# Sums of weights for the fast block products: made by adding transfers in device memory and loaded, in place of VectorE additions

## The reference

```
n2 = rms_norm(h)                      # 512 x 1024
a  = relu(n2 @ w_in) ** 2             # w_in 1024 x 4096
h  = h + a @ w_out                    # w_out 4096 x 1024
```

## Time and profile before

| what | value |
|---|---|
| median of 3 runs | 1870.49 us (1870.12 to 1870.89) |
| the profiled execution, its own time | 1871.36 us |
| its span | 1869.6 us |
| TensorE busy | 1858.5 us (99%) |
| VectorE busy | 1369.3 us (73%) |
| ScalarE busy | 944.1 us (50%) |
| GpSimd busy | 87.4 us (5%) |
| moved by DMA | 179.34 MB, mean 96 GB/s |

### The profile page before, as it was taken

One profiled execution on the slowest core, in us unless ns is written; L12 is line 12 of the kernel. 1 busy time (PEld: TensorE's weight loads), 2 busy tenths in 40 slices (PEclk: granted clock), 3 DMA queues, 4 the chain that ended last, 5 costly groups with the idle time before them and its releaser, 6 DMA issues.

```text
span 1869.6 us, 28250 instructions
## 1 busy us (share of the span) xinstructions
PE 1858.5 (99%) x10603; PEld 1546.0 (83%) x10603; DVE 1369.3 (73%) x1870; ACT 944.1 (50%) x1206; POOL 87.4 (5%) x84
## 2 busy tenths in 40 slices
PE   9999999999999999999999999999999999999998
PEld 7788878888888887877888898988778788989897
DVE  7767775677357667556577898987788658789887
ACT  6392464555133344444543554555667744445464
POOL 0010021000000021000100000000110010000000
PEclk9999999999999999999999999999999999999999
DMA  6223122332322234222233223234232133233321
GB/s 242 90 85 125 44 68 68 104 98 68 112 90 91 74 105 134 68 82 68 90 99 98 96 92 113 92 112 149 88 104 71 59 101 102 82 107 99 105 91 68
DMA packets 146802, 179.34 MB, mean 96 GB/s; under 512 B 3581, under 2 KB 140669, under 8 KB 144256
## 3 DMA queue, kind: packets, MB, share of 16 engines
q1 hardware_dynamic: 143296, 160.44, 26.4%
q0 software_dynamic: 3104, 17.10, 2.9%
q10 hardware_dynamic: 288, 0.26, 0.0%
HBM read 173.48 MB, written 2.20 MB: 94 GB/s over the span
## 4 chain that ended last, share of the span: by engine, by line
PE 92%; DVE 5%; ACT 2%; DMA 1%; issue 0%; DVEq 0%; SPq 0%; ACTq 0%
PE bank L1059 22%; PE bank L1061 22%; PE bank L1060 22%; PE bank L1496 4%; PE bank L1498 4%; PE bank L1497 4%; PE bank L1187 2%; PE bank L1801 2%; PE bank L1783 1%; PE bank L1193 1%; DVE w_lo L2061 1%; DMA raw<-in_mlp_w_out 1%; PE bank L1672 1%; PE bank L1673 1%; PE bank L1674 1%; DVE w_lo L1897 1%
## 5 line engine op out<-in xcount | busy, mean ns | idle before, releaser
L1059 PE MATMUL bank<-n_hi,w_hi 128*128 128x512 f32 x1054 | 424.7, 403 | 1.3 <-DVE w_lo L1897 1.3
L1061 PE MATMUL bank<-n_hi,w_lo 128*128 128x512 f32 x1054 | 417.9, 396 | 0.0
L1060 PE MATMUL bank<-n_lo,w_hi 128*128 128x512 f32 x1054 | 416.7, 395 | 0.0
L1891 ACT ACTIVATE w_hi<-raw 128x2048 fp32r<-128x2048 f32 (+2 forms) x115 | 215.0, 1870 | 342.1 <-PE bank L1061 337.5
L1897 DVE TENSOR_TENSOR w_lo<-raw,w_hi 128x2048 fp32r<-128x2048 f32 (+2 forms) x121 | 271.2, 2241 | 105.5 <-ACT w_hi L1891 103.4
L1060 PE MATMUL bank<-ff_lo,w_hi 128*128 128x512 f32 x752 | 297.2, 395 | 0.0
L1061 PE MATMUL bank<-ff_hi,w_lo 128*128 128x512 f32 x688 | 273.0, 397 | 0.0
L1059 PE MATMUL bank<-ff_hi,w_hi 128*128 128x512 f32 x688 | 271.5, 395 | 1.0 <-DVE ff_lo L2199 0.8
L1059 PEld LDWEIGHTS bank<-n_hi,w_hi 128*128 128x128 f32 x1054 | 198.0, 188 | 54.2 <-issue 5.0
L1060 PEld LDWEIGHTS bank<-n_lo,w_hi 128*128 128x128 f32 x1054 | 198.1, 188 | 48.9 <-issue 2.9
L1061 PEld LDWEIGHTS bank<-n_hi,w_lo 128*128 128x128 f32 x1054 | 197.9, 188 | 46.6
(11 more groups left out here) (455 smaller groups left out, 3111.1 us busy)
## 6 DMA issues: line engine op xcount, KB each, us to landing
raw<-in_mlp_w_in SPq DMA_DIRECT2D x32, 1024.0 KB, 5.4
raw<-in_mlp_w_out SPq DMA_DIRECT2D x32, 1024.0 KB, 5.1
raw<-in_w_up SPq DMA_DIRECT2D x22, 1024.0 KB, 5.0
raw<-in_w_units SPq DMA_DIRECT2D x14, 1024.0 KB, 4.8
raw<-in_a_w_qkv SPq DMA_DIRECT2D x12, 1024.0 KB, 5.1
raw<-in_b_w_qkv SPq DMA_DIRECT2D x12, 1024.0 KB, 5.1
b_bias<-bias_table POOLq DMA_DIRECT2D x16, 448.0 KB, 4.5
raw<-in_w_down SPq DMA_DIRECT2D x8, 768.0 KB, 4.4
```

What stands on the lines that cost most here:

```text
L1059: nc.tensor.matmul(b[:, :], w_hi[:, j % 2, cols], hi, start=start, stop=False)
L1060: nc.tensor.matmul(b[:, :], w_hi[:, j % 2, cols], lo, start=False, stop=False)
L1061: return nc.tensor.matmul(b[:, :], w_lo[:, j % 2, cols], hi, start=False, stop=final)
L1891: act.activation(w_hi[:, s, cols], raw[:, s, cols], ACT.Copy).then_inc(hi_ready, 1)
```

## The change

The two MLP weight matrices are handed over in blocks (`in_blocks`, on the host): for each unit a contiguous 128 x 2048 array whose row holds four blocks of 512 columns, in the order of `BLOCK_ORDER` (A21, A11, A12, A22 as (tile, far) pairs (1, 0), (0, 0), (0, 1), (1, 1)). A unit's row in memory is then 8 KB in one run, where it was 8 runs of 1 KB.

POOL gets a new piece of work, `weight_sums`, in two sets of 15 units. The first set stands behind `norm_pool(1)`, ahead of `attention_a_pool`; the second behind `norm_pool(4)`, ahead of `attention_b_pool`. For each unit it issues five transfers from device memory to device memory: two copies of two blocks (512 KB each), an adding transfer of two blocks, another of two blocks, and one of one block (256 KB). The four stages of a unit are spread over four steps, each step holds the stages of up to four units, and POOL waits at the start of a step until all transfers of the step before have landed. A set has 18 steps.

SP loads, for each of the 30 units, three blocks of the unit (768 KB, `raw[:, :, SEQ:4*SEQ]`) and its four sums (1024 KB) straight into `s_parts`. The load of the sums waits on SP for the sums to be made and for the place to be free. VectorE's three sum instructions are gone, and some signs are turned in the remaining additions (a subtraction in place of an addition, or `scalar_tensor_tensor` with -1). S1 and S4 change places. The plain products of these matrices read their columns in the new order.

```diff
+BLOCK_ORDER = ((1, 0), (0, 0), (0, 1), (1, 1))
+def in_blocks(w, rows, cols):
+    v = w.reshape(2, rows, KD // 2, 2, P, cols, 4, 2, P).transpose(0, 1, 5, 6, 4, 7, 3, 2, 8)
+    v = np.stack([v[:, :, :, :, :, tile, far] for tile, far in BLOCK_ORDER], 5)
+    return v.reshape(32, P, UNIT)
...
+        def block_loads(sp, ph):
+            m, is_out = block_phases[ph]
+            for j in range(4):
+                u = j if not is_out else DOWN if j == 2 else None
+                sp.wait_ge(lo_ready, ph.u0 + j - 1)
+                if u is None:
+                    sp.dma_start(raw[:, j % 2, :].rearrange("p (k n) -> p k n", n=GC).unsqueeze(1),
+                                 ph.view[:, j:j + 1, :, :]).then_inc(w_loaded[j % 2], 16)
+                    continue
+                sp.dma_start(raw[:, j % 2, SEQ:4 * SEQ], t["mlp_out" if is_out else "mlp_in"][4 * m + j, :, SEQ:4 * SEQ]).then_inc(
+                    w_loaded[j % 2], 16)
+                row = SUM_ROW[m, u]
+                sp.wait_ge(sums_made, 16 * sums_issued[row + 3, SUM_SETS[m // 4][0]])
+                if u == 0:
+                    sp.wait_ge(at("piece_lo"), split_count[m - 1, "operand", OPERANDS - 1] if m % 4 == 1 else split_count[m - 1, "S14", DOWN])
+                elif u == 1 and m % 4 > 1:
+                    piece_used(sp, m - 1, ("S3", DOWN))
+                elif u > 1:
+                    sp.wait_ge(at("piece_lo"), split_count[m, "S14", 2 if u == DOWN else u - 2])
+                i = sums_place(u)
+                sp.dma_start(s_parts[i], t["weight_sums"][row]).then_inc(sums_loaded[i], 16)
...
+            def copied(row):
+                v, to = source(row), sums(row)
+                pool.dma_start(to[:, 0:2, :], v[:, 1:2, :].broadcast_to([P, 2, SEQ])).then_inc(sums_made, 16)
+                pool.dma_start(to[:, 2:4, :], v[:, 2:4, :]).then_inc(sums_made, 16)
+            def first_added(row):
+                pool.dma_start(sums(row)[:, 1::2, :], source(row)[:, 0:1, :].broadcast_to([P, 2, SEQ]), accum_op=ALU.add).then_inc(sums_made, 16)
+            def second_added(row):
+                pool.dma_start(sums(row)[:, 0:4:2, :], sums(row)[:, 3:4, :].broadcast_to([P, 2, SEQ]), accum_op=ALU.add).then_inc(sums_made, 16)
+            def third_added(row):
+                pool.dma_start(sums(row)[:, 2:3, :], source(row)[:, 1:2, :], accum_op=ALU.add).then_inc(sums_made, 16)
+            for step in range(first, last + 3):
+                if step > first:
+                    pool.wait_ge(sums_made, 16 * sums_issued[step - 1, first])
+                for back, part in enumerate((copied, first_added, second_added, third_added)):
+                    if first <= step - back < last:
+                        part(step - back)
+            pool.wait_ge(sums_made, 16 * sums_issued[last + 2, first])
...
             norm_pool(pool, 1)
+            weight_sums(pool, *SUM_SETS[0])
             pool.wait_ge(at("bias_stored"), 16)
             attention_a_pool(pool)
             norm_pool(pool, 4)
+            weight_sums(pool, *SUM_SETS[1])
             attention_b_pool(pool)
...
-            own_dve(dve, dve.tensor_tensor(halves(unit_rows(u)[:, 1, :]), halves(z[:, :]), twice(third_row(u)), ALU.add))
+            own_dve(dve, dve.scalar_tensor_tensor(halves(unit_rows(u)[:, 1, :]), halves(z[:, :]), -1.0, twice(third_row(u)), ALU.mult, ALU.subtract))
...
-            if has_down(m):
-                paired_sums(dve, m, DOWN)
-                second_sum(dve, m, DOWN)
-                fourth_sum(dve, m, DOWN)
             unit_low(dve, m, UNITS - 1)
             split_lo(dve, p_dn[m].u0 + 1, 1)
```

More of the change, by code:

```diff
@@ L818, in piece_used, with sums_place, summed @@
             eng.wait_ge(at("piece_used"), piece_count[(m,) + piece])
-        def summed(eng, m, u, n):
-            eng.wait_ge(at("sums_ready"), sum_count[m, u, n])
+        SUM_ROW = {}
+        for m in range(8):
+            for u in range(BLOCKS if has_down(m) else UNITS) if m % 4 else ():
+                SUM_ROW[m, u] = len(SUM_ROW)
+        assert len(SUM_ROW) == SUM_UNITS
+        sums_loaded, sums_made = [sem("sums_loaded0"), sem("sums_loaded1")], sem("sums_made")
+        SUM_SETS = ((0, SUM_UNITS // 2), (SUM_UNITS // 2, SUM_UNITS))
+        sums_issued, issued = {}, 0
+        for first, last in SUM_SETS:
+            for step in range(first, last + 3):
+                issued += sum(n for back, n in enumerate((2, 1, 1, 1)) if first <= step - back < last)
+                sums_issued[step, first] = issued
+        def sums_place(u):
+            return u % 2 if u < UNITS else 0
+        def summed(eng, m, u):
+            i = sums_place(u)
+            eng.wait_ge(sums_loaded[i], 16 * sum(sums_place(v) == i and n <= SUM_ROW[m, u] for (_, v), n in SUM_ROW.items()))
         def places_free(eng, m, op, u):
@@ L906, in weight_loads @@
                     round_(it, False)
+        block_phases = {ph: (m, is_out) for is_out, own in enumerate((p_in, p_dn)) for m, ph in enumerate(own)
+                        if m % 4 and (has_down(m) or not is_out)}
+        def block_loads(sp, ph):
[17 more added lines that the diff above has]
+                    sp.wait_ge(at("piece_lo"), split_count[m, "S14", 2 if u == DOWN else u - 2])
+                i = sums_place(u)
+                sp.dma_start(s_parts[i], t["weight_sums"][row]).then_inc(sums_loaded[i], 16)
         def input_part(eng, i):
@@ L929, in _ @@
             for ph in phases:
[L930 removed]
+                if ph in block_phases:
+                    block_loads(sp, ph)
+                else:
+                    weight_loads(sp, ph)
             for c in range(TOK):
@@ L999, in shifts_of, with weight_sums, source, sums @@
             return bass.AP(tensor=table.tensor, offset=row * RB_COLS + at0, ap=[[1, P], [RB_COLS, rows], [1, n]])
+        def weight_sums(pool, first, last):
+            def source(row):
+                m, u = list(SUM_ROW)[row]
+                v = t["mlp_in"][4 * m + u] if u < UNITS else t["mlp_out"][4 * m + 2]
+                return v.rearrange("p (b n) -> p b n", n=SEQ)
+            def sums(row):
+                return t["weight_sums"][row].rearrange("p (b n) -> p b n", n=SEQ)
+            def copied(row):
[8 more added lines that the diff above has]
+                pool.dma_start(sums(row)[:, 2:3, :], source(row)[:, 1:2, :], accum_op=ALU.add).then_inc(sums_made, 16)
+            for step in range(first, last + 3):
+                if step > first:
[4 more added lines that the diff above has]
+            pool.wait_ge(sums_made, 16 * sums_issued[last + 2, first])
         def attention_a_pool(pool):
```

96 lines of the change are left out of this document (36 added, 60 removed).

## The result

The changed kernel takes **1875.27 us** (median of 11 runs, 1873.12 to 1879.38); the kernel before, on the same chip, 1870.38 (11 runs, 1869.66 to 1870.89). The ratio is 1.0027, with a 95% interval of 1.0017 to 1.0036. So the change makes the kernel 4.9 us slower, where I had forecast 1868.5 and "same": inside my range of 1866 to 1885, on the other side of the sign.

What follows compares the result with a forecast made beforehand. TensorE, busy 1858.5 of 1869.6 us, was taken as the bound. Less 2.0 us for its removed waits, nothing for the rest: span 1869.3, for a median 1868.5 us ("same"); own range 1866.5 to 1872, 8-in-10 range 1866 to 1885.

Steps and rivals of the forecast that it cites:

- What is removed: VectorE's sums, 78.4 us, go; TensorE gets back only its waits in the plain products between burst and `DOWN`: -2.0 us.
- Rival 4: At the plain products ahead of `DOWN`, `unit_low` waits for ScalarE about as long instead: 1870.5 us, chance 0.05.
- What is moved on SP: SP's queue carries 23.6 MB more in rows of 6 or 8 KB, with 13 us of cover: costs nothing.
- The price of an addition: In POOL's transfers an added block costs two copied: 18.9 us a step, not 13.1; 302 us a set, not 215.
- What is added on POOL: 150 transfers in two idle stretches of POOL, 349.75 and 345.78 us; both sets fit beside the loads at next to no cost.
- My 18.1 us: Cover of one load of `raw` beside POOL's transfers: place free at 348.02, needed at 366.11.
- rival 2: Loads of weights crowded out by POOL's transfers, each unit 2.1 us behind, some 50 us a set: 1970 us, chance 0.07.
- The second set: POOL's sums ahead of layer B's tables: some 350 us, ending 5 us behind POOL's present start; next to no cost.
- rival 1: POOL's sets don't fit and hold up what follows, from 21.8 us a step; 2110 us at 30 a step, chance 0.14.

Runs made afterwards that it cites:

- experiment 1: The changed kernel without POOL's transfers in device memory, SP loading the unit's own weights in place of the sums: 1868.03 us, ratio 0.9987.
- Experiments 9 and 10: The kernel before with `unit_low` ahead of VectorE's sums of `DOWN`, 1877.64 us; with the split of `DOWN`'s second unit ahead too, 1881.74 us.
- experiments 5 and 6: `w_up`, `w_down` and `b_w_qkv` handed over in rows of 6 or 8 KB: in the changed kernel 1868.05 us, in the kernel before 1869.95 us.
- experiment 3: The changed kernel with the second set of sums alone, the other half loading the unit's own weights: 1873.27 us, ratio 1.0016.
- after: The changed kernel with the whole change, against the kernel before: 1875.27 us in the median, 1873.12 us in its profiled execution.
- experiment 2: The changed kernel with the first set of sums alone, the other half loading the unit's own weights: 1868.81 us, ratio 0.9996.

## Why the prediction was wrong, point by point

- **What is removed: right.** -2.0 us forecast; all six stretches went to 22.40 us, and experiment 1, with the gain alone, is 2.4 us under the kernel before (0.7 to 4.1). Rival 4 (the wait comes back) is out. Experiments 9 and 10 add what I had not looked at: that the order before was the best of those tried.
- **What is moved on SP: right.** 23.6 MB more cost nothing (experiment 1).
- **The price of an addition: right.** 302 us for the first set against 298, a share of 0.60 + 0.28 = 0.88 against 0.92 measured. A byte in an adding transfer costs 1.7 copied ones and not 2.
- **The step that failed first** is the one that followed, in "What is added on POOL": "a share of 0.60, so both fit". It took the sum of two shares under 1 to mean that the loads of weights land as before. They landed in 10.3 us in the median and 19.3 at most, with engines that were not full. I had the right cover in mind only for one kind of load. My 18.1 us are those of a 1 MB unit of w_up, 48 matmuls long. The load of w_down that came late was issued at 478.79, and TensorE wanted its unit at 496.79 + 0.23 = 497.02. Less the two passes over it (1.92 + 2.30) and the gaps between, it had to land within 13.8 us; it took 15.5. A unit of 768 KB is 36 matmuls, 8.4 us, not 11.2. That is my rival 2, which I gave 0.07 at a price of 100 us: the mechanism is there, in single loads and not in all, and it costs 1.8 us. The rule of the Trainium skill that I cited beside it, packet by packet, was right about who loses, and experiments 5 and 6 agree with it; I let the arithmetic of shares outvote it.
- **The second set: a term mis-sized at a threshold.** I had it at 350 us, ending 5 us behind POOL's present start, "next to nothing". It took 360, and b_lam came 15.7 us late. Up to 11.8 us late is free (experiment 3), so 5 would indeed have cost nothing, and the ten us by which the sum was short turned nothing into a stall (4.0 us in experiment 3's trace, with the lower clock behind it). The steps beside the bursts were not what was short. POOL's timeline of after has the first step beside the burst of m = 1, and the first of the last three, start here:

```profile
1006.85 0.75 POOL L1067 DMA_DIRECT2D weight_sums<-in_mlp_in  x1 [23.39 <-DMA weight_sums<-in_mlp_in]
...
1237.48 1.04 POOL L1071 DMA_DIRECT2D weight_sums<-in_mlp_out  x1 [20.55 <-DMA weight_sums<-in_mlp_in]
```

  Between them are ten steps, 230.6 us, 23.1 each (17.8 to 27.8), where I had 23.7. From 916.00 to 1006.85 it is 90.9 us, where I had 94.5. The last three steps took 1275.97 - 1237.48 = 38.5 us, where I had 3 x 6.2 = 18.6. The code has not fifteen full steps and three short ones, but three that fill, twelve full and three that drain, and those that drain still write 2304 KB, all of it added. That is the term of the sum that was mis-sized. In the first set the same count did no harm (302 for 298). The late end is the largest part of the loss, 5.3 of 7.2 us. This is rival 1, which I gave 0.14 for a time of 2110, with its deciding point worked out (21.8 us a step) but no price for passing it by little.
- **The sum**: -2.4 + 1.8 + 5.3 = +4.7 us against the kernel before, measured +4.9. My terms for the last two were both 0. The stated range, 1866 to 1885, held the time because I had stretched it for a set late by some 10 us, which is about what came; the forecast of 1868.5 and its own range, up to 1872, did not. I had called the second set "the thinnest cover of the change" and gave slower 0.21. A sum of 350 us that is good to a few per cent, and whose limit is 357.6 (345.78 + 11.8), should have had nearer to even chances.

## What to carry to other kernels

A transfer that is "hidden" has two covers to be checked: its own deadline, and the landing times of every other load that shares the engines, each against the shortest cover of its kind; two shares that add up to less than 1 say nothing of the second. Where background traffic must run beside loads, give the loads long rows first: it cost nothing here by itself, and beside the transfers the kernel got back all 7 us, some 2 by loads that landed in time and the rest by a second set that ended sooner, for a reason that is open. Count the steps of a pipeline one by one, its draining steps too. And before moving work off an engine, look whether it stands in a hole of that engine: 78 us of VectorE were worth 2.4, because 76 of them were in nobody's way.

## What the runs showed of the hardware that I had not expected

- A transfer within device memory that adds took 1.7 times the engine time of a copy per byte, not 2 (53.1% and 38.0% of the engines for the same 35.39 MB, in 14640 and 9840 packets).
- With the engines 0.92 busy, loads in 1 KB rows landed in 10.3 us for 5.0, at most 19.3 for 6.4; with rows of 6 and 8 KB in 7.3, at most 13.3. With free engines the rows made no such difference: 4.7 us for 5.0.
- A stall of TensorE of 4.0 us was followed by 3.4 us at 1.2 GHz (granted clock 0.66 over 5 us), which cost 1.5 us more; the four stalls of after, 0.8 to 1.7 us, and one of 3.1 in experiment 2, were not followed by such a stretch.
- The spread is a sign too: the kernel before and the kernels in which nothing is late vary by 0.8 to 1.8 us over eleven runs, those with a set that can be late by 4.2 to 6.3.

Open are why the second set was 14 us shorter with long rows, and what the profile of a typical run of after, 2 us above the one shown, would show.
